# Step sizes and running sums in another form, merged rows transposed inside the projections, embedding and second-bias products moved into experts 22 to 27

## The reference, cut to what matters

```
h = rms_norm(x);  proj = h @ w_in  ->  u | v | z | xBC | dt | gate_a | gate_b
y_a = u * (W_s @ layer_norm(v) + b)                      # spatial gating, 8 groups of 128x128
xBC = silu(causal_depthwise_conv(xBC));  dt = softplus(dt + bias);  a_dt = -exp(a_log) * dt
a_cs = cumsum(a_dt)                                      # within chunks of 128 tokens, 16 heads
decay[q, s] = exp(where(q >= s, a_cs[q] - a_cs[s], -inf))
y_diag = (C B^T * decay) @ (x dt);  y_off through the state of the first chunk
y_b = rms_norm((y_diag + y_off + D x) * silu(z))
merged = sigmoid(gate_a) * (y_a @ Wa) + sigmoid(gate_b) * (y_b @ Wb)
x1 = x + merged @ w_out
logits -> top 4 of 32 experts, softmax of the four
x2 = x1 + sum over experts of gate * (swiglu(rms(x1) @ w1[e] + b1[e]) @ w2[e] + b2[e])
x3 = x2 + sigmoid(rms(x2) @ w_ple_gate) * (p @ w_ple_proj)
out = rms_norm(x3)
```

## Time and profile before

| | us |
|---|---|
| median of 3 runs | 1261.99 (1261.02 to 1265.23) |
| profiled execution | 1265.43 |
| its span | 1263.5 |
| PE busy | 1219.7 (97%) |
| DVE busy | 398.3 (32%) |
| ACT busy | 222.8 (18%) |
| copies | 457.24 MB, mean 362 GB/s |

### The profile page before, as it was taken

How to read it: one execution, slowest core, us unless ns; L and a number is a source line. 1 busy time by engine, 2 the same in 40 slices (tenths; PEclk the granted TensorE clock), 3 DMA queues, 4 the chain that set the end, 5 groups by cost and what they waited for, 6 DMA issues and landing times.

```text
span 1263.5 us, 15417 instructions
## 1 busy us (share of the span) xinstructions
PE 1219.7 (97%) x6327; PEld 653.8 (52%) x6327; DVE 398.3 (32%) x716; ACT 222.8 (18%) x313; POOL 45.0 (4%) x32
## 2 busy tenths in 40 slices
PE   8999999989999999999999999999999999999987
PEld 7988788866444444444444444433334443333326
DVE  2769764543111221221122112111112221112126
ACT  4755454442000000000000000000000000000027
POOL 6600000010000000000000000000000000000000
PEclk9989999997999999999999999999999999999999
DMA  9644447937899999999999999999999999999990
GB/s 283 203 141 133 131 149 307 355 138 306 365 429 425 430 428 428 430 427 429 430 426 430 429 427 430 428 428 430 426 430 428 427 430 429 427 430 426 430 364 34
DMA packets 61742, 457.24 MB, mean 362 GB/s; under 512 B 7305, under 2 KB 16881, under 8 KB 37138
## 3 DMA queue, kind: packets, MB, share of 16 engines
q1 hardware_dynamic: 61714, 456.84, 87.9%
HBM read 455.77 MB, written 1.05 MB: 362 GB/s over the span
## 4 chain that ended last, share of the span: by engine, by line
PE 72%; DMA 24%; DVE 2%; issue 1%; ACT 1%; SPq 0%; DVEq 0%; ACTq 0%
PE bank L940 22%; DMA wring<-in_w_dram 18%; PE bank L993 13%; PE bank L902 7%; DMA vz<-in_w_dram 6%; PE bank L661 6%; PE bank L662 5%; PE bank L663 5%; PE bank L911 3%; PE bank L948 1%; PE bank L712 1%; PE bank L719 1%; PE bank L715 1%; PE bank L648 1%; PE bank L970 1%; PE bank L918 1%
## 5 line engine op out<-in xcount | busy, mean ns | idle before, releaser
L940 PE MATMUL bank<-wring,hT 128*64 128x512 f32 x1376 | 309.5, 598 | 12.3 <-DMA wring<-in_w_dram 11.5
L940 PEld LDWEIGHTS bank<-wring,hT 128*64 128x64 f32 x1376 | 95.4, 137 | 206.5 <-issue 177.7
L1743 DVE TENSOR_SCALAR xbcT<-bank 128x512 f32<-128x512 f32 x32 | 22.2, 692 | 436.8 <-PE bank L948 436.8
L993 PE MATMUL bank<-wring,xbcT 128*64 128x512 f32 x688 | 155.9, 601 | 0.6 <-DVE xbcT L1756 0.6
L902 PEld LDWEIGHTS bank<-xbcT,ga 128*128 128x128 f32 x1024 | 121.6, 195 | 3.9 <-DVE xbcT L1706 1.2
L902 PE MATMUL bank<-xbcT,ga 128*128 128x64 f32 x1024 | 120.4, 277 | 0.9 <-DVE xbcT L1706 0.9
L1276 ACT ACTIVATE xbcT<-xbcT 128x512 f32<-128x512 f32 x32 | 20.2, 630 | 512.6 <-DVE xbcT L1743 512.6
L993 PEld LDWEIGHTS bank<-wring,xbcT 128*64 128x64 f32 x688 | 47.9, 138 | 103.7 <-issue 102.9
L1758 DVE COPY xbcT<-bank 128x256 f32<-128x256 f32 x32 | 13.6, 424 | 265.6 <-PE bank L918 265.6
L1404 DVE TENSOR_TENSOR blk_lo<-blk,blk_hi 128x2048 fp32r<-128x2048 f32 x32 | 73.1, 2289 | 53.7 <-ACT blk_hi L1100 53.7
L1281 ACT ACTIVATE xbcT<-bank 128x512 f32<-128x512 f32 x32 | 19.1, 597 | 362.5 <-PE bank L993 362.5
(11 more groups left out here) (272 smaller groups left out, 1131.4 us busy)
## 6 DMA issues: line engine op xcount, KB each, us to landing
wring<-in_w_dram SPq DMA_DIRECT2D x129, 2048.0 KB, 33.1
blk<-in_w_dram SPq DMA_DIRECT2D x42, 2048.0 KB, 32.7
vz<-in_w_dram SPq DMA_DIRECT2D x21, 2048.0 KB, 32.9
blk<-in_w_in_dram SPq DMA_DIRECT2D x28, 1024.0 KB, 5.1
blk<-in_w_branch_a_dram SPq DMA_DIRECT2D x4, 1024.0 KB, 5.1
blk<-in_w_branch_b_dram SPq DMA_DIRECT2D x4, 1024.0 KB, 8.7
blk<-in_w_out_dram SPq DMA_DIRECT2D x4, 1024.0 KB, 5.2
x<-in_x_dram SPq DMA_DIRECT2D x4, 512.0 KB, 5.1
```

Source lines behind the costliest of these rows:

```text
L940: last = mm(bank[dh * SLOTS:(dh + 1) * SLOTS, :], xgT[:, k, :], at(c)[:, kk * 2 * F + off + dh * W:kk * 2 * F + off + (dh + 1) * W], start ...
L993: last = mm(YB[dh * SLOTS:(dh + 1) * SLOTS, :], actT[:, kk * P + c * SLOTS:kk * P + (c + 1) * SLOTS], at(W1C + c)[:, kk * D + dh * W:kk * ...
L1743: ts(g_sb, GLU[:, :], LIMIT, None, ALU.min).then_inc(g_done, 1)
```

## The change

- **Step sizes.** dt is computed transposed: the high and low parts of its weights lie side by side (32 columns) as the stationary operand, and the high and then the low part of the activations stream past with 256 columns, 16 products instead of 48. ScalarE copies the result out (`dtT`), and after the first row half of v two small float32 products with `dsel` add the parts and turn them back (`time_steps`).
- **Running sums.** Two small float32 products give the sums transposed (`acsT`, 16 rows). ScalarE copies them out, SP stores them to main memory behind the load of half 16 and, behind the load of half 17, loads them back spread over all partitions, 1 MB for each chunk (`acs_spread`). VectorE takes the minimum with the own sum (four instructions of 128x1024), ScalarE takes 32 exponentials of 128x128 with the negated own sum as bias. The seg products and `segments` are gone. VectorE's layer norm of v is four instructions instead of six, and the multiplication by D moves behind the decays.
- **Merged rows.** The left halves of the merged rows are transposed inside wb (after its first row half of block 1), the right halves inside wo (after its first quarter of block 0); wo waits for each piece when it needs it. VectorE's `weight_low(38, 39)` comes after the splitting of the merged rows. Half of the logits moves inside wo.
- **Embedding.** Only the transposes of p stay before the experts, after the logits. The eight products run in experts 24 to 27 in bank LIN, behind the scatter; ScalarE copies each result.
- **Second bias.** The four products leave expert 0; VectorE sets the accumulating banks to zero, and experts 22 and 23 add the products.
- **Copies.** Chunk 0 is loaded after `y_done` behind half 24, chunks 1 and 2 behind halves 29 and 31, w_ple_proj behind half 28. The first quarter of w_ple_gate goes ahead of the last chunk.
- **End.** TensorE reads the number of overflows before the last expert, and the last scatter stands before the branch. ScalarE splits the second quarter of w_ple_gate after the transposed rows. Experts 1 to 21 are the loop, 22 to 31 are written out.

```diff
+LOOPED = 21
+EMBED_AT = {24: (0, 0), 25: (0, 1), 26: (1, 0), 27: (1, 1)}
+BIAS_AT = {22: 0, 23: 1}
...
+                if i == HALF_OF["z", 0, 0]:
+                    wait_taken(sp, ("acsT",))
+                    load(acs_rows.rearrange("c (h q) -> h c q", h=HEADS), acsT.rearrange("h (c q) -> h c q", c=TT), acs_stored)
+                if i == HALF_OF["z", 0, 1]:
+                    sp.wait_ge(acs_stored, 16)
+                    for c in range(TT):
+                        load(decay[c].rearrange("p h q -> p (h q)"), acs_rows[c, :].partition_broadcast(P), acs_spread[c])
...
+                if i == HALF_OF["gb", 0, 0]:
+                    sp.wait_ge(y_done, TT)
+                    load_chunk(0)
                 if i in (FIRST_WA + 1, FIRST_WA + 3):
 
-                    load_chunk((i - FIRST_WA) // 2)
-                if i == FIRST_WA + NB + 1:
-                    sp.wait_ge(y_done, TT)
-                    load_chunk(2)
-                if i == HALF_OF["wb", 0, 0]:
-                    sp.wait_ge(yssq_done, TT)
+                    load_chunk((i - FIRST_WA) // 2 + 1)
...
+            for g in range(NCH * (E - GROUP), NCH * E):
+                if g == NCH * E - 1:
+                    sp.wait_ge(chunk_used, NCH * E - NSLOT + 1)
+                    load_gate(0, 0)
+                sp.wait_ge(chunk_used, g - NSLOT + 1)
+                load_chunk(g)
+            load_gate(0, 1)
+            sp.wait_ge(chunk_used, NCH * E - NSLOT + 2)
+            load_gate(1, 0)
+            load_gate(1, 1)
...
-            for t in range(TT):
+            wait_empty(pe, ("dtT",))
+            for part in (a_hi, a_lo):
                 for k in range(KT):
-                    cols, heads = slice(t * P, (t + 1) * P), slice(k * HEADS, (k + 1) * HEADS)
-                    last = three(bank_of(("dt",))[:, t * HEADS:(t + 1) * HEADS], (a_hi[:, k, cols], a_lo[:, k, cols]),
-                                 (wdt_hi[:, heads], wdt_lo[:, heads]), k == 0, k == KT - 1)
-            last.then_inc(full(("dt",)), 1)
-            natural("v", a_hi, a_lo)
+                    last = mm(bank_of(("dtT",))[0:2 * HEADS, 0:TOKENS], wdt2[:, k].rearrange("p a h -> p (a h)"), part[:, k, :],
+                              start=(part is a_hi and k == 0), stop=(part is a_lo and k == KT - 1))
+            last.then_inc(full(("dtT",)), 1)
+            def time_steps():
+                pe.wait_ge(dsel_set, 1)
+                wait_taken(pe, ("dtT",))
+                wait_empty(pe, ("dt",))
+                for t in range(TT):
+                    last = mm(bank_of(("dt",))[:, t * HEADS:(t + 1) * HEADS], dtT[:, t * P:(t + 1) * P], dsel[:, :],
+                              start=True, stop=True)
+                last.then_inc(full(("dt",)), 1)
+            natural("v", a_hi, a_lo, [0], time_steps)
+            natural("v", a_hi, a_lo, [1])
...
+            wait_empty(pe, ("acsT",))
+            for c in range(TT):
+                last = mm(bank_of(("acsT",))[0:HEADS, c * P:(c + 1) * P], adt[:, c, :], upper[:], start=True, stop=True)
+            last.then_inc(full(("acsT",)), 1)
...
-            for c in range(TT):
-                for g in range(GROUPS):
-                    name = ("seg", c, g)
-                    wait_empty(pe, name)
-                    for r in range(HPG):
-                        h = g * HPG + r
-                        last = mm(bank_of(name)[:, r * P:(r + 1) * P], bcast(adt[:, c, h:h + 1], [P, P]), upper[:],
-                                  start=True, stop=True)
-                    last.then_inc(full(name), 1)
...
+            def merged_rows(h):
+                for t in range(TT):
+                    pe.wait_ge(merged, TT * h + t + 1)
+                    transposes(("mT", t, h), [ga[:, t, (4 * h + i) * P:(4 * h + i + 1) * P] for i in range(4)])
+            def after_wb(b, kh, t):
+                if (b, kh, t) == (1, 0, 1):
+                    merged_rows(0)
...
-            pe.wait_ge(p_loaded, 16)
-            transposes(("pT",), [p_nat[:, t, k * P:(k + 1) * P] for k in range(2) for t in range(TT)])
-            pe.wait_ge(wpp_loaded, 16)
-            wait_taken(pe, ("pT",))
-            def embed(b, t):
-                dense(("pp", b, t), [pT[:, k, t * P:(t + 1) * P] for k in range(2)],
-                      [wpp[:, k, b * W:(b + 1) * W] for k in range(2)])
-            embed(0, 0)
-            embed(0, 1)
-            for t in range(TT):
-                pe.wait_ge(merged, TT + t + 1)
-                for h in range(2):
-                    transposes(("mT", t, h), [ga[:, t, (4 * h + i) * P:(4 * h + i + 1) * P] for i in range(4)])
-            embed(1, 0)
...
+            def taken(kh, t):
+                wait_taken(pe, ("mT", t, kh))
+            def after_wo(b, kh, t):
+                if (b, kh, t) == (0, 0, 0):
+                    merged_rows(1)
+                if (b, kh, t) == (1, 0, 1):
+                    for r in range(TT):
+                        residual(r, 0)
+                if (b, kh, t) == (1, 1, 0):
+                    pe.wait_ge(wr_scaled, 1)
+                    wait_empty(pe, ("logit",))
+                    for r in range(TT):
+                        logits(r, 0)
+            natural("wo", b_hi, b_lo, ready=taken, after=after_wo)
             residual(0, 1)
-            logits(0, 0)
             residual(1, 1)
-            logits(1, 0)
             logits(0, 1)
             logits(1, 1).then_inc(full(("logit",)), 1)
-            embed(1, 1)
+            pe.wait_ge(p_loaded, 16)
+            transposes(("pT",), [p_nat[:, t, k * P:(k + 1) * P] for k in range(2) for t in range(TT)])
...
-                if first:
-                    pe.wait_ge(b2_loaded, 16)
-                    wait_taken(pe, ("wo", 1, 1), ("logit",), ("pp", 1, 1), ("rank",))
-                    for t in range(TT):
-                        for dh in range(2):
-                            mm(ACC[t][dh][:, :], gateT[:, t * P:(t + 1) * P], b2_all[:, dh * W:(dh + 1) * W],
-                               start=True, stop=True)
+                if first or alone:
+                    pass
                 elif last_one:
 
                     selected(GLU)
                 else:
                     scatter(lambda: None)
+                if extra is not None:
+                    extra()
...
+            def second_bias(dh):
+                pe.wait_ge(b2_loaded, 16)
+                for t in range(TT):
+                    mm(ACC[t][dh][:, :], gateT[:, t * P:(t + 1) * P], b2_all[:, dh * W:(dh + 1) * W],
+                       start=False, stop=True, skip_group_check=True)
+            def embed(b, t):
+                pe.wait_ge(wpp_loaded, 16)
+                for k in range(PLE // P):
+                    last = mm(LIN[:, :], pT[k][:, t * P:(t + 1) * P], wpp[:, k, b * W:(b + 1) * W],
+                              start=(k == 0), stop=(k == PLE // P - 1))
+                last.then_inc(embed_filled, 1)
+            wait_taken(pe, ("rank",))
             streamed(0, 0, first=True)
-            with pe.Fori(0, (E - 2) // GROUP) as i:
+            pe.wait_ge(acc_zeroed, 1)
+            with pe.Fori(0, LOOPED // GROUP) as i:
                 for r in range(1, GROUP + 1):
                     streamed(GROUP * i + r, r, i)
-            streamed(E - 1, E - 1, last_one=True)
+            for j in range(LOOPED + 1, E - 1):
+                extra = None
+                if j in BIAS_AT:
+                    extra = lambda: second_bias(BIAS_AT[j])
+                if j in EMBED_AT:
+                    extra = lambda: embed(*EMBED_AT[j])
+                if j - 1 in EMBED_AT:
+                    pe.wait_ge(embed_done, list(EMBED_AT).index(j - 1) + 1)
+                streamed(j, j, extra=extra)
             pe.wait_ge(extra_done, 1)
             n = pe.value_load(n_extra[0:1, 0:1], min_val=0, max_val=OVF - 1)
+            streamed(E - 1, E - 1, last_one=True)
+            pe.wait_ge(y_copied, E)
+            pe.wait_ge(selT_done, E)
+            for t in range(TT):
+                for dh in range(2):
+                    last = mm(ACC[t][dh][:, :], selgT[dh * SLOTS:(dh + 1) * SLOTS, t, :],
+                              y_sb[dh * SLOTS:(dh + 1) * SLOTS, :], start=False, stop=True, skip_group_check=True)
+                last.then_inc(acc_done, 1)
...
-                for g in range(GROUPS):
-                    wait_taken(act, ("seg", c, g))
-                    d = decay[c][:, g * HPG:(g + 1) * HPG, :]
-                    fn(d, d, ACT.Exp).then_inc(dexp_done, 1)
+                act.wait_ge(nacs_done, 1)
+                for h in range(HEADS):
+                    if h % 8 == 0:
+                        act.wait_ge(bounded, 2 * c + h // 8 + 1)
+                    last = fn(decay[c][:, h, :], decay[c][:, h, :], ACT.Exp, bias=nacs[:, c, h:h + 1])
+                    if h % HPG == HPG - 1:
+                        last.then_inc(dexp_done, 1)
...
+                if j in EMBED_AT:
+                    b, t = EMBED_AT[j]
```

(45 more changed lines are left out.)

177 lines of the change are left out of this document (97 added, 80 removed).

## The result

The changed kernel takes 1233.18 us, median of four runs (1231.99 to 1234.83), against 1261.51 us, median of four runs of the kernel before (1260.64 to 1265.23). The ratio is 0.9767 with a 95% interval of 0.9745 to 0.9789: faster by 2.3%, 28.3 us. The forecast of 1228.5 was 4.7 us too low, inside its range of 1221 to 1240.

A forecast was written before the change was run, and what follows sets the result against it. Time was taken as first chunk use, set by TensorE's front, plus fixed weight copying with gaps, plus a tail. Front -28.8, hidden work +0.5, gap -3.2, late experts 0, tail -2.3 and +0.2: -33.6 from 1262.0, 1228.4 (likeliest 1228.5), range 1221 to 1240.

The forecast's parts named there:

- dt: Step sizes ahead of v: 16 wide products and four small float32 ones replace 48 thin products, -3.5 us.
- seg: Mamba stage before z: segment products removed, -7.2 us, and TensorE's pause behind them, -2.2 us.
- wb to wo: Wait between wb and wo for merged rows goes, 16 transposes stay: -10.2 us; clock dip at wo's start, -1.7.
- the gap: Copy pause before chunk 13 in expert 0 shrinks from 3.6 to 0 to 0.8 us without second-bias products: -3.2 us.
- the tail: After the last expert: branch behind the last scatter, -2.3 us; w_ple_gate quarter loaded ahead of the last chunk, +0.2.
- The rival that it would be replaced: At wo, a late merge or split leaves half of the 10.2 us and the clock dip: +6.8, 1235 us; 9%.
- rival 5: Change brings nothing: the front's gain ends in waiting for chunks 6 to 8; 2%.
- Logits and routing: Between wo and expert 0: `rank` starts earlier without the last embedding block, -1.1 us; moved logits half, +0.9.
- rival 3: TensorE enters expert 0 at 1.2 GHz and stays there, using chunks slower than they are copied: +11, 1240 us; 6%.
- Experts 22 to 27: Moved embedding and bias products: up to 0.55 us behind per expert, 1.25 won back in each of 28 to 30: 0.
- rival 4: Experts written out: TensorE stalls on new code, slower overall from 5 us per expert, 1269 us at 6; 2%.
- the way to be most wrong: Stream starts on time but ends late, by a copy gap or slower rate in experts 22 to 31; no size given.

The follow-up runs named there:

- Experiments 5 and 6: changed kernel with extra products ahead of v, 32 thin (16 columns) or 35 dense (256 columns): 1244.18 and 1241.61 us.
- experiment 3: changed kernel with the running sums formed as before (16 segment products, eight exponentials, no store or spread loads): 1246.8 us, ratio 0.9875.
- the second execution: kernel before, unchanged, profiled once more: 1262.45 against 1262.78 us, ratio 0.9993; this profiled execution took 1264.97 us, span 1263.0.
- experiment 2: changed kernel with the splitting of the merged rows put back behind the last three halves of wo's weights: 1246.25 us, ratio 0.987.
- Experiments 9 and 10: changed kernel with unread products filling TensorE's waits between logits and expert 0, twelve of 512 columns or three float32: 1230.75 and 1229.19 us.
- experiment 7: changed kernel with the second-bias products back in expert 0 and none in experts 22 and 23: 1237.15 us, ratio 0.9798.
- experiment 8: changed kernel with the embedding products of experts 24 to 27 computed twice: 1236.48 us, ratio 0.9793.
- Experiment 12: changed kernel with the count's reading and the branch back between the last expert and its last scatter: 1232.83 us, ratio 0.9772.
- experiment 11: changed kernel with 32 never-executed products added inside the overflow branch that is not taken: 1239.68 us, ratio 0.9813.

## Why the prediction was right, and where not

The total came out inside the range by the mechanism forecast for the large terms (dt, seg, wb to wo, the gap), with two terms too hopeful by about 1 and 2 us, and with one, the tail, that came out by luck.

**What bounds the kernel** held in its consequence: the time moved by what the front, the gap and the tail gave. One sentence did not. It said that from 314 on a copy is under way nearly always and that TensorE only waits; in fact TensorE sets the pace (27.81 us per expert) for half of the experts, using up the chunks loaded ahead, and the copies (29.36) only for the rest. It still takes an earlier start through whole, since both paces start there.

**The mamba stage.** In the prediction's own terms, with the four small products counted under dt, dt gave 3.0 for 3.5 and the clock in v 2.0 for 2.2. Experiments 5 and 6 show that the thin products are the cause of such a dip, at a price of 1.5 for 32 of them. seg with its pause gave 9.6 for 9.4 and the dip in z 1.6 for 1.6; the segment products are 7.3 of it, and experiment 3 shows that the rest belongs to the change as a whole. The spread loads landed after 7.4 and 9.4 us (8 taken), VectorE waits 2.72 for the first, and z starts 0 late, not 0.5. ScalarE's 32 exponentials:

```profile
L1272 ACT ACTIVATE wring<-wring,nacs x32: 385/388/403, 120.5 to 129.6; 128x128 f32<-128x128 f32 x32
```

Duration in ns, then first and last start: 9.1 us for 31 of them, 0.294 each, 9.5 in all. The bounds from rows were 6.4 and 12.8; the estimate from "ScalarE: Activation LUTs", "What ACT_TABLE_LOAD costs", in the Trainium skill was 9.4, and the trace agrees. They are hidden, as forecast.

**wb to wo** gave 11.5 with the logits for 11.0 (9.8 against the second execution, in which wo started without a dip), and experiment 2 gives 11.9 back by the first gather. The rival that it would be replaced fell, and so did rival 5: TensorE waits for no chunk before expert 16.

**Logits and routing** is the first term that failed: -1.1 forecast, 0.0 measured, -0.7 against the second execution. The step said that `rank` starts earlier once the embedding block is gone. Counted from the logits it does, by 1.05 us, against the profiled execution; in the second, where the block ran at full clock, `rank` started no later than in the changed kernel (2.14 us after the logits in both). What the step left out is the clock behind. From 275 to 285 us it is 0.50, and the gather takes 7.0 to 7.1 us in all ten traces of changed kernels without filling, against 6.26 and 6.97 in the two of before. From `rank` to the gather it is 2.8 us here, but 2.2 to 3.0 in other kernels with the same code up to there, and 2.1 and 2.2 before. So the low clock is there in both kernels, and how much of it comes from the missing block, two executions of before can't say. It is the mechanism of rival 3, which was priced only as 11 us inside expert 0. Experiments 9 and 10 show the whole price of the low clock here, 5.3 us, most of which the kernel before paid as well: its clock was 0.50 too from 305 to 310, in both executions.

**The gap** gave 4.3 for 3.2 against the profiled execution, and experiment 7 gives the same 4.3 back; against the second execution of the kernel before (11.8 us between the chunks) it is 2.6. The term was right within what this place varies.

**Experts 22 to 27** is the second term that failed: 0 forecast, 1.8 measured. The falling behind was right (0.36 us in each of six, 0.55 allowed, 2.2 in all). The step that failed is "wins back 1.25 in each of experts 28, 29, 30", and with it "the copies queue up many chunks ahead and lose nothing". TensorE's waits for chunks in experts 28 and 29:

```profile
1121.16 3.65 PE L986 MATMUL bank<-wring,hT 128*64 128x512 f32 x16 [0.74 <-DMA wring<-in_w_dram]
...
1150.52 3.65 PE L986 MATMUL bank<-vz,hT 128*64 128x512 f32 x16 [1.24 <-DMA vz<-in_w_dram]
```

0.6 us are won back and then the wait for the copies is as long as ever. The rest can't be won back, because the copies themselves are late by then. In the kernel before each chunk from the twentieth on lands 4.84 to 4.95 us after the one ahead of it. In the changed kernel three land late, chunk 155 most (chunks counted from 0; start of the issue, and time from there to the landing):

```profile
970.48 0.33 SPq L600 DMA_DIRECT2D wring<-in_w_dram  x1
DMA to landing us min/median/max: 36.7/36.7/36.7
973.91 0.33 SPq L600 DMA_DIRECT2D wring<-in_w_dram  x1
DMA to landing us min/median/max: 39.1/39.1/39.1
```

That is 1007.2 and 1013.0, 5.8 us apart, and with chunks 145 and 161 1.5 us in all. From the last chunk of expert 21 to that of expert 30 it is 264.3 and 264.4 us in the two traces of before, and 265.8 to 266.1 in all twelve others, whether the late experts have no bias products (experiment 7) or the embedding twice (experiment 8). So the loss isn't set by what TensorE is given to do there. Among the things that those twelve have in common is that experts 22 to 31 are written out. Copies of the changed kernel from 900 to 1140 us (queue: packets, MB, share):

```profile
q8 instruction: 10, 0.16, 0.3%
```

Ten instruction packets come in this stretch; in the kernel before, none does. That these packets make the weight copies late is a guess: no run separates them from the rest of the change. It would be rival 4's cause (new code in the written-out experts) by another way and at 1.5 us in all. It is also what the prediction named as the way to be most wrong, a stream that starts on time and ends late. In experiment 8 the lag was so great that the copies stayed ahead to the end, and 4.6 us were won back.

**The tail** gave 2.8 for 2.1 (3.2 against the second execution) and is right for a wrong reason, which is luck. The wait ahead of the last scatter is 0.70 us instead of 2.91 and the scatter 1.9 instead of 3.5; of these 3.8 us 0.2 go to the last w2 products, 7.28 us instead of 7.09, as forecast for the load ahead of them, and 0.7 are lost behind the scatter. The step said that reading the count and branching cost 2.26 us ahead of the last scatter and would be covered behind it. Experiment 12 puts them back and nothing is lost; experiment 11 changes nothing but the place of the code and some 6 us are lost. In the kernel before, a packet of the instruction queue lies between 1224.6 and 1227.4, in the idle stretch of the earlier trace rows itself. So by all that the runs show this gain comes from where the code behind the branch lies, not from the order that the diff changes; on the kernel before itself it was not tried. This cause had no place in the prediction; rival 4 named code as a cost, but as a stall of TensorE at the experts written out, and no such stall shows. (Its price for 6 us per expert is also a slip: 9 x (6 - 1.25) - 33.6 = +9.2 gives 1271, not 1269.)

**The difference to the median.** The terms come to 31.3 instead of 33.6 (30.8 against the second execution). The other 3 us of 28.3 against 31.3 lie in the executions profiled: those of the kernel before were 3.9 and 2.5 above the medians of their runs. Which stage these are in I can't say.

## What to carry to other kernels

Where TensorE waits ahead of a stage on the path, look at the clock of that stage: here filling the waits with three long products that nobody reads brought its start 5.3 us forward. And profile the kernel before twice ahead of a forecast, since in one profile the same stage was 0.7 to 1.7 us longer or shorter than in the other. A pause that nothing releases right behind a branch was code loading here; it came and went with how much code lay ahead, so an edit anywhere can add or remove some 4 us there, and two versions should be compared by stages and not by their total alone. In a stream with a lead, write down both paces, the engine's and the copies', before saying what an added instruction costs, and look at when the copies land, not only at the waits for them.
